# Grid attention of a two-block transformer kernel: inverse sums multiplied into the head pairs' outputs, and seven of sixteen turned-probability evictions on VectorE

## The reference, cut to what matters

```
s_loc = einsum("bwhd,brwkhd->bhwrk", q_r, k_win) * scale + bias
s_ctx = einsum("bwhd,bchd->bhwc", q_r, k_ctx) * scale
scores = concatenate([s_loc.reshape(bsz, nh, GRID_W, n_loc), s_ctx], axis=-1)
p = softmax(scores, axis=-1)
return (einsum("bhwrk,brwkhd->bwhd", p_loc, v_win)
        + einsum("bhwc,bchd->bwhd", p_ctx, v_ctx))
...
x = x + g1 * (concatenate([attn, y_ssd], axis=-1) @ w_out)
```

## Time and profile before

| what | value |
| --- | --- |
| median of 3 runs | 1004.91 us |
| span of the profiled execution, first to last instruction | 1003.8 us |
| TensorE busy | 964.3 us (96%) |
| VectorE busy | 690.0 us (69%) |
| ScalarE busy | 517.5 us (52%) |
| grid attention, first S to end of O3 | 708.4 to 778.5 us of the span |
| TensorE idle from 742 to 772 us | 7.3 us of 30 |

### The profile page before, as it was taken

How to read it: one execution, slowest core, us unless ns; L and a number is a source line. 1 busy time by engine, 2 the same in 40 slices (tenths; PEclk the granted TensorE clock), 3 DMA queues, 4 the chain that set the end, 5 groups by cost and what they waited for, 6 DMA issues and landing times. The chain is left out here.

```text
span 1003.8 us, 14808 instructions
## 1 busy us (share of the span) xinstructions
PE 964.3 (96%) x5812; PEld 826.2 (82%) x5812; DVE 690.0 (69%) x968; ACT 517.5 (52%) x715; POOL 53.0 (5%) x71
## 2 busy tenths in 40 slices
PE   7989999999999999999999999999987989999997
PEld 4468898998977877889999887889855789999996
DVE  2576658999855666647778674466677787777775
ACT  2466575445546565555444554454556454444443
POOL 0310000000001110000000000000001000000000
PEclk9999999999999999999999999999998999999999
DMA  9122575867665742677888561332210536555541
GB/s 363 65 95 97 214 266 213 282 222 284 233 219 178 237 143 85 215 276 275 325 336 306 198 252 58 111 122 88 85 43 1 193 130 222 184 179 181 183 173 42
DMA packets 28943, 185.04 MB, mean 184 GB/s; under 512 B 3680, under 2 KB 4384, under 8 KB 9312
## 3 DMA queue, kind: packets, MB, share of 16 engines
q1 hardware_dynamic: 23472, 155.54, 42.9%
q0 software_dynamic: 4416, 28.31, 7.8%
q10 hardware_dynamic: 1008, 0.55, 0.2%
HBM read 181.76 MB, written 2.62 MB: 184 GB/s over the span
## 5 line engine op out<-in xcount | busy, mean ns | idle before, releaser
L2006 DVE TENSOR_TENSOR split<-raw,split 128x2048 fp32r<-128x2048 f32 x122 | 279.6, 2292 | 177.6 <-ACT split L1446 175.9
L1446 ACT ACTIVATE split<-raw 128x2048 fp32r<-128x2048 f32 x121 | 231.5, 1913 | 235.9 <-PE bank L724 192.9
L722 PE MATMUL bank<-acts,split 128*128 128x256 f32 (+1 forms) x960 | 278.1, 290 | 2.2 <-DVE acts L2046 1.4
L724 PE MATMUL bank<-acts,split 128*128 128x256 f32 (+1 forms) x960 | 276.7, 288 | 0.0
L723 PE MATMUL bank<-acts,split 128*128 128x256 f32 (+1 forms) x960 | 276.7, 288 | 0.0
L722 PE MATMUL bank<-split,acts 128*128 128x512 f32 (+1 forms) x544 | 211.7, 389 | 2.8 <-DVE split L2006 1.9
L723 PE MATMUL bank<-split,acts 128*128 128x512 f32 (+1 forms) x544 | 208.8, 384 | 0.0
L724 PE MATMUL bank<-split,acts 128*128 128x512 f32 (+1 forms) x544 | 208.6, 383 | 0.0
L722 PEld LDWEIGHTS bank<-acts,split 128*128 128x128 f32 x960 | 183.7, 191 | 9.6 <-issue 3.1
L723 PEld LDWEIGHTS bank<-acts,split 128*128 128x128 f32 x960 | 183.8, 191 | 3.4
L724 PEld LDWEIGHTS bank<-acts,split 128*128 128x128 f32 x960 | 183.7, 191 | 1.9
(11 more groups left out here) (248 smaller groups left out, 1033.9 us busy)
## 6 DMA issues: line engine op xcount, KB each, us to landing
raw<-w_mlp SPq DMA_DIRECT2D x64, 1024.0 KB, 4.8
raw<-w_glu SPq DMA_DIRECT2D x22, 1024.0 KB, 4.8
bias<-w_ada POOLq DMA_DIRECT2D x14, 1024.0 KB, 7.0
raw<-w_qkv SPq DMA_DIRECT2D x12, 1024.0 KB, 5.6
arena<-w_glu_down SPq DMA_DIRECT2D x22, 512.0 KB, 3.3
work<-w_ada POOLq DMA_DIRECT2D x10, 1024.0 KB, 5.9
raw<-w_mla_o SPq DMA_DIRECT2D x4, 1024.0 KB, 5.1
raw<-w_moba_o SPq DMA_DIRECT2D x4, 1024.0 KB, 4.7
```

Of the source, the lines that this page charges most:

```text
L722: pe.matmul(out_, a[0], b[0], start=first, stop=False)
L724: return pe.matmul(out_, a[1], b[0], start=False, stop=last)
L1446: return act.activation(out_, in_, ACT.Copy)
L2006: v.tensor_tensor(split[:, c % 2, 1, 0:n], raw[:, c % 2, 0:n], split[:, c % 2, 0, 0:n].bitcast(F32), ALU.subtract).then_inc(lo_ready, 1)
```

## The change

- `window_normalise` is gone. P is released by the exponential itself (its `small_free`), and turns unnormalised probabilities.
- The row sums go to eight columns of `stat`. After steps 3, 7, 11 and 15 `invert_sums(p)` takes the reciprocal of a pair's four sums at once.
- A new TensorE piece R before each O: four matmuls of 128 columns, the inverse sums repeated over 64 columns as the stationary side and the identity as the moving side, so that row 64e + d of a bank of the small ring holds the inverse sum of each token. R takes a unit of that ring, so later units sit in other banks.
- A new VectorE piece `pair_scaled(p)`: copies R's bank to SBUF (128 x 256), waits for O, and multiplies `pair_bank` by it into `pair_rows`. It runs in steps 4, 8 and 12, and for the last pair between `rows_means` and `rows_scaled`. `pair_out` and `pair_lo` read `pair_rows`; `pair_lo(3)` now stands behind `rows_scaled`.
- For steps 0, 4, 5, 7, 8, 10 and 11 VectorE evicts P (`turned(i)`, right after `window_logits(i + 2)`) in place of ScalarE.

```diff
+TURNED = (0, 4, 5, 7, 8, 10, 11)
...
         if i in WEIGHTED:
+            steps.append(("R", WEIGHTED.index(i)))
             steps.append(("O", WEIGHTED.index(i)))
-    steps.append(("O", 3))
+    steps += [("R", 3), ("O", 3)]
...
                 elif kind == "P":
-                    pe.wait_ge(probs_ready, 2 * H + i + 1)
+                    small_gone(pe, window_unit("S", i))
...
+                elif kind == "R":
+                    u = window_unit(kind, i)
+                    small_start(u)
+                    pe.wait_ge(sums_inverted, i + 1)
+                    for t in range(2):
+                        for e in range(2):
+                            ins = pe.matmul(sbank(u)[64 * e:64 * e + 64, t * P:(t + 1) * P],
+                                            repeated(stat[:, :], 360 + 4 * (i % 2) + 2 * t + e, 64), ident, start=True,
+                                            stop=True)
+                    ins.then_inc(small_ready, 1)
...
             out_chunk(0, 0, (0,))
+            grid_work("R", 3)
             grid_work("O", 3)
             out_chunk(0, 0, (1, 2))
-            pe.wait_ge(pair_free, 4)
+            pe.wait_ge(pair_split, 4)
             out_chunk(0, 0, (3,))
...
-                act.wait_ge(pair_ready, p + 1)
-                copy(acts[:, 0, 0, p * T:(p + 1) * T], pair_bank[:, 0:T]).then_inc(out_hi, 1)
+                act.wait_ge(pair_free, p + 1)
+                copy(acts[:, 0, 0, p * T:(p + 1) * T], pair_rows[:, p % 2, :]).then_inc(out_hi, 1)
...
-                if i:
+                if i and i - 1 not in TURNED:
                     turned_out(i - 1)
...
-            def window_normalise(i):
...
+            def turned(i):
+                h, t = head_and_tokens(i)
+                u = window_unit("P", i)
+                small_out(v, u)
+                v.tensor_copy(view(att, 2048 + 1024 * (h % 2), 4, T)[:, :, t * P:(t + 1) * P],
+                              sbank(u)[:, :].rearrange("p (a b) -> p a b", a=4)).then_inc(small_free[u % 4], 1)
+            def invert_sums(p):
+                for i in range(4 * p, 4 * p + 4):
+                    small_gone(v, window_unit("S", i))
+                a = 4 * (p % 2)
+                v.reciprocal(stat[:, 360 + a:364 + a], stat[:, 352 + a:356 + a]).then_inc(sums_inverted, 1)
+            def pair_scaled(p):
+                u = window_unit("R", p)
+                small_out(v, u)
+                v.tensor_copy(inverse_rows[:, p % 2, :], sbank(u)[:, 0:T]).then_inc(small_free[u % 4], 1)
+                small_gone(v, u)
+                v.wait_ge(pair_ready, p + 1)
+                v.tensor_tensor(pair_rows[:, p % 2, :], pair_bank[:, 0:T], inverse_rows[:, p % 2, :], ALU.mult).then_inc(pair_free, 1)
...
             for i in range(2 * H):
-                window_normalise(i)
                 if i + 2 < 2 * H:
                     window_logits(i + 2)
+                if i in TURNED:
+                    turned(i)
+                if i % 4 == 3:
+                    invert_sums(i // 4)
                 if i in CARRIED:
                     carried_rows(CARRIED.index(i))
                 if i - 1 in DECAY:
                     matrix(DECAY.index(i - 1))
...
                 if i == 4:
                     used(GC["z"])
+                if i in (4, 8, 12):
+                    pair_scaled(i // 4 - 1)
                 if i in (5, 9, 13):
                     pair_lo(i // 4 - 1)
...
             rows_means()
+            pair_scaled(3)
+            rows_scaled()
             pair_lo(3)
-            rows_scaled()
```

More of the change, by code:

```diff
@@ L86 @@
          ("cum", 1), ("cumcol", 1), ("later", 1), ("xsrow", 4), ("brow", 1),
-         ("state", 2), ("cb", 2), ("nq", 2), ("nk", 1), ("na", 35), ("d2", 4)]
+         ("state", 2), ("cb", 2), ("nq", 2), ("nk", 1), ("na", 39), ("d2", 4)]
 def plan():
@@ L213, in grid_order @@
             n += 2
-        if kind in ("P", "T", "K"):
+        if kind in ("P", "T", "K", "R"):
             units[(kind, i)] = n
@@ L340, in program @@
         h0T = view(work, 5120, 2, NA)
+        pair_rows, inverse_rows = view(arena, 13824, 2, T), view(arena, 1536, 2, T)
         gact = view(arena, 1024, 2, T)
@@ L411, in program @@
         max_ready, exp_done, probs_ready = sem("max_ready"), sem("exp_done"), sem("probs_ready")
+        sums_inverted, pair_split = sem("pair_sums_inverted"), sem("pair_low_parts")
         silu_c, squared = sem("silu_c"), sem("relu_squared")
@@ L1293, in grid_work @@
                 elif kind == "O":
-                    for m in range(4 * i, 4 * i + 4):
-                        small_gone(pe, window_unit("P", m))
                     if i == 0:
@@ L1299, in grid_work @@
                         pe.wait_ge(pair_free, i)
+                    for m in range(4 * i, 4 * i + 4):
+                        small_gone(pe, window_unit("P", m))
                     for k in range(4):
@@ L1353, in _ @@
                 grid_work(kind, i)
-            for kind, i in steps_w[:-1]:
+            for kind, i in steps_w[:-2]:
                 grid_work(kind, i)
@@ L1371, in out_chunk @@
                     ins.then_inc(down_used, 1)
-            pe.wait_ge(pair_free, 3)
+            pe.wait_ge(pair_split, 3)
             pe.wait_ge(y_free, 1)
@@ L1838, in window_exp @@
                 act.activation(att[:, 512 * (i % 4):512 * (i % 4) + 512], sbank(u)[:, :], ACT.Exp, scale=-1.0,
-                               bias=stat[:, 56 + i % 4:57 + i % 4], accum_out=stat[:, 60 + i % 4:61 + i % 4])\
+                               bias=stat[:, 56 + i % 4:57 + i % 4], accum_out=stat[:, 352 + i % 8:353 + i % 8])\
                     .then_inc(small_free[u % 4], 1)
@@ L2668, in window_logits @@
                                        op0=ALU.add, op1=ALU.min, accum_out=stat[:, 56 + b:57 + b]).then_inc(max_ready, 1)
-            def window_normalise(i):
[L2671 to L2676, removed]
+            def turned(i):
[16 more added lines that the diff above has]
+                v.tensor_tensor(pair_rows[:, p % 2, :], pair_bank[:, 0:T], inverse_rows[:, p % 2, :], ALU.mult).then_inc(pair_free, 1)
             def pair_lo(p):
                 v.wait_ge(out_hi, 2 * H + p + 1)
-                v.tensor_tensor(acts[:, 0, 1, p * T:(p + 1) * T], pair_bank[:, 0:T],
+                v.tensor_tensor(acts[:, 0, 1, p * T:(p + 1) * T], pair_rows[:, p % 2, :],
                                 acts[:, 0, 0, p * T:(p + 1) * T].bitcast(F32), ALU.subtract)\
-                    .then_inc(pair_free, 1)
+                    .then_inc(pair_split, 1)
             def matrix(h):
@@ L2703, in carried_rows @@
                 tm = arena[:, 1024:1536]
+                settle()
                 v.wait_ge(ecum_ready, 1)
```

## The result

The changed kernel took 1011.13 us (median of 4 runs, 1009.29 to 1011.17) against 1005.22 us before: a ratio of 1.0053, interval 1.0041 to 1.0065, so 5.3 us slower by the ratio (the medians are 5.9 apart). A second comparison with five rounds gave 1.0055 (1.0043 to 1.0067). The forecast was +4.0 us, in a range of 1005.0 to 1011.8 us. The first profiled execution is the fastest of its four: span 1007.5 us, where the other three have 1009.3 to 1009.4.

A forecast was written before the change was run, and what follows sets the result against it. TensorE bounds most of the kernel, but the touched stage is bound by a ring of in-order engines waiting for each other. Order and tail +2.7 plus clock +1.3 give +4.0: 1004.91 to 1008.9 us, range 1005.0 to 1011.8.

The forecast's parts named there:

- Step 4: VectorE's copy waits for P4; split, pair product and logits 7 queue behind it, so S4 comes 3.9 us later.
- Steps 0 to 3: Stage start: `turned(0)` holds VectorE at no cost; S3 loses its 0.91 us wait, R0 adds 0.95, P4 stays.
- Steps 5 to 15: Rest of the stage: S4-S5 -0.4, S5-S6 +1.1, S6-S7 -0.1; 3.4 us given back after S7, last eviction +1.0.
- R: Price of the new TensorE piece before each O: 0.95 us each, bounds 0.7 and 1.3, taken from Y's form.
- Tail: After the means, `pair_scaled(3)` and `rows_scaled` run before `pair_lo(3)`, so TensorE's last piece comes later: +1.7 us.
- Clock: One fall of TensorE's granted clock behind the 4.0 us wait before S4: +1.3 us, bounds 0 and 2.7.
- The old fall: Kernel before: half clock around P11 and S7, costing O2 1.7, Y5 0.8 and S7 0.2, together 2.7 us.
- rival 2: Two clock falls, one as forecast and one at the old place before S7: +6.7 us, 1011.6; chance 0.17.
- order, at full clock in both: Whole stage and tail: the new engine order's cost with no clock fall in either kernel, +5.4 us.
- The 1.1 us that I put around a span: Whole execution: time outside the profiled span, 1.1 us added to the predicted span of 1007.8.
- Rivals 3 and 4: Third: P4's delay absorbed as logits 7 catches up, +1, chance 0.14. Fourth: faster overall, -1.3, chance 0.11.
- Rival 4: Ring: VectorE's multiply was the only slow link; waits and clock fall go with it, -1.3 us, 1003.6; chance 0.11.

The follow-up runs named there:

- e1: Changed kernel with step 4's weight split moved before VectorE's copy `turned(4)`; ratio 1.0025 to the kernel before.
- e4: Changed kernel with all sixteen evictions of turned probabilities on ScalarE again, inverse sums and R kept; 1003.9 us, ratio 0.9978 to the kernel before.
- e7: Changed kernel with only step 4's eviction back on ScalarE, six left on VectorE; ratio 1.0000 to the kernel before.
- e10: Changed kernel with idle-time matmuls on TensorE in three waits (before S4, the G of step 10 and S7); ratio 1.0011 to the kernel before.
- e3: Changed kernel with the last pair's pieces moved earlier: R3's copy before `rows_means`, `pair_lo(3)` before `rows_scaled`; ratio 1.0043 to the kernel before.
- e9: Changed kernel run again unmodified, on the same chip and in the same rounds as its version with fillers; ratio 1.0055 to the kernel before.
- e12: Kernel before the change with idle-time matmuls in three waits (before F2, P11 and S7); ratio 0.9969 to that kernel without them.
- the reordered one: Changed kernel with no eviction on VectorE, pair products one step later and the last pair's pieces earlier; ratio 0.9948 to the kernel before, 0.9922 with fillers.
- e5: Changed kernel with 8 idle-time matmuls on TensorE before S4; ratio 1.0046 to the kernel before.

## Why the prediction was right, and where it was not

**Step 4, right.** `turned(4)` waited for P4 behind O0, the split and the first pair's product ran behind it, and logits 7 came after them. Predicted for S3 to S4: 743.2 less 730.4, 12.8 us. Measured: 12.43. e1, e4 and e7 show the cause, not only the place.

**Steps 0 to 3, right.** S3 came 0.9 us earlier, as said. The 5.5 us for which VectorE stood before `turned(0)` cost nothing seen on TensorE: S2 and the first pieces of Z are at the same distance from the first S.

**Steps 5 to 15, close.** With the clock at full speed in e10, S4 to S5, S5 to S6 and S6 to S7 took 6.26, 8.34 and 8.12 us; predicted 6.4, 8.9 and 8.0, where the 8.9 has an R at twice its price. S7 to the last piece: predicted 784.75 less 766.5, 18.25; e10 17.92.

**R, too dear.** I took 0.95 us and the row says 0.49 of TensorE's time; the bound of 0.7 was wrong too. R is like an O in form (a stationary side of 64 columns, 128*64 in the row), and an O's sixteen passes of 256 columns take 1.9; Y, from which I took it, loads 128 columns for each pass. The rows of the weight loads bear this out: R's eight loads take 0.41 us, Y's eight 1.09. R0, R1 and R2 lie on the path: 1.4 us too much.

**Tail, right.** Predicted +1.7 for its order. From the means to the last piece it is 2.27 us where it was 0.55, so 1.72; e3 takes 1.5 us of it back.

**Clock, the direction right and the size wrong.** I forecast one fall for 1.3 us and gave two falls 0.17. There are two in the first profile, in e9 and, as a short and a long one, in e1. e10 prices them at 4.4 us together. The old fall I had at 2.7 from its rows; e12 makes it 3.1. So rival 2's mechanism is what happened, and the number still lay between it (+6.7) and the forecast (+4.0) because the order was over-priced. That the sum came out within 1.5 us was in part luck: the order was 1.2 us too dear and the clock of the changed kernel 3.1 us too cheap. The sum in the prediction's terms (the measured ones are differences of ratios, so they close by construction; as the execution profiled in e12 still had a short fall, and not every execution of e10 was at full clock throughout, both clock terms are lower bounds):

| term | predicted | measured | from |
| --- | --- | --- | --- |
| order, at full clock in both | +5.4 (2.7 + 2.7) | +4.2 | e10 to e12 |
| clock, changed kernel | +1.3 | +4.4 | e9 to e10 |
| clock, kernel before | -2.7 | -3.1 | e12 |
| sum | +4.0 | +5.5 | e9: 1.0055 |

The 1.1 us that I put around a span was wrong too: in the changed kernel it is 1.8 (1009.29 less 1007.5), as in most executions here. With 1.8 the profile before belongs to a time near 1005.6, the slowest of the three, and not to the median.

The rule of the Trainium skill that I set beside rival 2 (TensorE: Matmul & The Clock Gate, "A second HAM failure mode: psum-queue depth-cycling") tells of another kernel, in bf16, whose clock goes up and down because of short idle times between groups of matmuls. It was the better guide here than the one row at full clock from 742 to 748 of the kernel before. e10 to e12 agree with it as far as the idle times go: each of the three orders gained 2.6 to 4.4 us by filling its waits. That the going round the banks has a part in it, no run here shows.

**Rivals 3 and 4, wrong.** Nothing was absorbed: S4 followed exponential 7 at once. Rival 4's mechanism is half true, though. The multiply was a slow link: e4, which has no eviction on VectorE but keeps R and the slow tail, is 2.2 us faster than the kernel before, and its P14 waits 0.30 us and not 1.41. The size, -1.3, came near by luck: the rival counted the waits before S7 and the fall of the clock as gone, and in e4 TensorE waits 1.84 us before S7 and the clock falls twice, while R costs half of what the rival charged.

## What to carry to other kernels

Before work is moved to an engine that has time, look what the moved instruction waits for and what stands behind it in that engine's order: one copy of 0.69 us cost 5.3 us, because it made VectorE wait for Z3, R0 and O0 of TensorE (5.13 us) with a 2.3 us split and the next logits queued after it, and because the clock fell behind the wait; six others like it cost 2.2 us together. In a stage of short bursts price the waits twice, once as time and once as clock, and test the second part by filling the waits with matmuls that nobody needs. Compare orders with the clock held up in both, or the difference is partly which wait the fall happened to follow.

## What the runs showed of the hardware that was not expected

Matmuls that do nothing made a kernel faster: 4.4 us in the changed kernel, 3.1 us in the one before, 2.6 us in the reordered one (0.9948 to 0.9922, intervals 0.9928 to 0.9967 and 0.9909 to 0.9934, which touch, and from different sets of rounds, so the last size is the least sure). The added matmuls take 6.7, 4.1 and 3.8 us by their rows.

The granted clock fell to 0.50 after waits of 3.94 us, but also around waits of 1.38 and 1.84 us. A wait of 1.74 us in e1 had a fall behind it. The same wait of 1.50 us before F2 left the clock at full speed in the kernel before, and F2 took 1.13 us; in e4 the clock had fallen, and F2 took 2.08. From these rows alone it can't be said where a fall begins. First the kernel before, then e4:
```profile
743.98 1.13 PE L1324 MATMUL bank<-work,arena 128*128 128x256 f32 x4 [1.50 <-ACT arena L1857]
```
```profile
743.03 2.08 PE L1338 MATMUL bank<-work,arena 128*128 128x256 f32 x4 [1.50 <-ACT arena L1872]
```
In the profiles of e5 and e7, which have no first fall, the second is long (O2 3.63 us), but so it is in e1 and e9, which have both; that one fall taken away lengthens the next is not shown.

One product of the inverse sums, R, is nearly as cheap as the four transpositions of a P: it holds TensorE for 0.49 us (eight passes of 128 columns with 64 stationary columns) where P4 holds it for 0.41.
